# Second-layer weight sums of the MLP made by DMA in DRAM ahead of time, and one signal for each inner weight sum

## The reference

```
h    = rmsnorm(x); proj = h @ w_in
att  = sparse attention over the 256 best keys (prompt; sample with a paged cache)
rwkv = recurrent branch (delta-rule state, chunks of tokens)
x    = x + (sigmoid(gate_a) * (att @ w_branch_a) + sigmoid(gate_b) * (rwkv @ w_branch_b)) @ w_out
x    = x + square(relu(rmsnorm(x) @ w_mlp_in)) @ w_mlp_out        # 1024 -> 4096 -> 1024
y    = rmsnorm(x)
```

## Time and profile before

| | us |
|---|---|
| runs shown | 2499.18, 2497.75, 2504.57 (median 2499.18) |
| the profiled execution, its own time | 2501.81 |
| its span | 2500.0 |
| PE busy | 2294.0 (92%) |
| DVE busy | 1619.0 (65%) |
| ACT busy | 806.7 (32%) |
| POOL busy | 466.4 (19%) |
| DMA moved | 306.77 MB, mean 123 GB/s |

### The profile page before, as it was taken

One profiled execution on the slowest core, in us unless ns is written; L12 is line 12 of the kernel. 1 busy time (PEld: TensorE's weight loads), 2 busy tenths in 40 slices (PEclk: granted clock), 3 DMA queues, 4 the chain that ended last, 5 costly groups with the idle time before them and its releaser, 6 DMA issues. The chain is left out here.

```text
span 2500.0 us, 48830 instructions
## 1 busy us (share of the span) xinstructions
PE 2294.0 (92%) x19275; PEld 1709.7 (68%) x19275; DVE 1619.0 (65%) x3005; ACT 806.7 (32%) x1425; POOL 466.4 (19%) x354
## 2 busy tenths in 40 slices
PE   6999999999898999897999889999899999999986
PEld 4566788765656566665665668787687778778765
DVE  3257888964556564336557656648975785786787
ACT  4235888333343342224454432121121111111001
POOL 0020000000000000001101101034444544535441
PEclk8989999999999999899999999999999999999999
DMA  6441222443232313237877744506226325315302
GB/s 186 120 117 62 77 90 70 130 152 90 58 100 58 96 46 97 83 106 217 288 235 263 231 171 154 167 22 199 79 64 183 107 63 178 114 56 180 119 1 80
DMA packets 270656, 306.77 MB, mean 123 GB/s; under 512 B 56231, under 2 KB 183048, under 8 KB 270301
## 3 DMA queue, kind: packets, MB, share of 16 engines
q1 hardware_dynamic: 195316, 252.78, 32.0%
q10 hardware_dynamic: 75112, 50.87, 7.2%
HBM read 239.78 MB, written 62.23 MB: 121 GB/s over the span
## 5 line engine op out<-in xcount | busy, mean ns | idle before, releaser
L1286 PE MATMUL rwkv_banks<-gate_sides_then_att_T 128*128 128x384 f32 (+1 forms) x768 | 281.4, 499 | 8.4 <-PEq L441 3.7
L1286 PEld LDWEIGHTS rwkv_banks<-gate_sides_then_att_T 128*128 128x128 f32 x768 | 139.5, 197 | 77.1 <-issue 18.9
L3595 DVE TENSOR_TENSOR merged_then_hidden<-merged_then_hidden,ps_mm 128x544 f32<-128x544 f32 x180 | 127.5, 715 | 94.5 <-PE ps_mm L3320 94.5
L3320 PE MATMUL ps_mm<-gate_sides_then_att_T,w_mm 128*128 128x272 f32 x568 | 140.8, 397 | 10.1 <-issue 6.2
L600 PE MATMUL first_banks<-hT,w_pr 128*128 128x384 f32 (+3 forms) x432 | 144.3, 491 | 3.8 <-PEq L188 3.8
L910 DVE TENSOR_SCALAR_CACHE_REDUCE _and_tildes_then_k_pages<-scores,mid 128x384 f32<-128x384 f32 (+4 forms) x150 | 131.4, 876 | 3.1
L3320 PEld LDWEIGHTS ps_mm<-gate_sides_then_att_T,w_mm 128*128 128x128 f32 x568 | 108.6, 192 | 34.4 <-issue 7.0
L3402 ACT ACTIVATE merged_then_hidden<-merged_then_hidden 128x1088 f32<-128x1088 f32 x32 | 35.5, 1111 | 280.5 <-DVE merged_then_hidden L3607 280.5
L600 PEld LDWEIGHTS first_banks<-hT,w_pr 128*128 128x128 f32 (+1 forms) x432 | 81.1, 192 | 61.4 <-issue 20.5
L3320 PE MATMUL ps_mm<-gate_sides_then_att_T,w_sums_mm 128*128 128x272 f32 x400 | 101.3, 398 | 15.8 <-issue 6.8
L2376 POOL MEMSET gate_sides_then_att_T<- 128x136 f32 x1 | 0.2, 212 | 610.7 <-POOLq L1181 610.7
(11 more groups left out here) (619 smaller groups left out, 5289.4 us busy)
## 6 DMA issues: line engine op xcount, KB each, us to landing
v_pages<-in_cache_v SPq DMA_DIRECT2D x128, 256.0 KB, 5.3
gate_sides_then_att_T<-in_w_in ACTq DMA_DIRECT2D x46, 512.0 KB, 4.2
_and_tildes_then_k_pages<-in_cache_k SPq DMA_DIRECT2D x88, 256.0 KB, 3.4
gate_sides_then_att_T<-right_blocks_d SPq DMA_DIRECT2D x82, 272.0 KB, 2.8
right_blocks<-right_blocks_d SPq DMA_DIRECT2D x65, 272.0 KB, 2.7
T_and_gates_then_weights<-in_w_mlp_in SPq DMA_DIRECT2D x16, 1024.0 KB, 5.3
T_and_gates_then_weights<-in_w_mlp_out SPq DMA_DIRECT2D x16, 1024.0 KB, 5.4
w_pr<-in_w_in SPq DMA_DIRECT2D x27, 512.0 KB, 5.3
```

The source lines that it names most:

```text
L1286: ins = MM(B[:, gate_bank(n), 0:w], gw[:, n % 2, k_, :], hc[:, k_, 0:w], start=(k_ == 0), stop=(k_ == KO - 1))
L3320: ins = nc.tensor.matmul(ps[:, bank, 0:272], w, right[:, k, :], start=(k == 0 and step in f.OPENS), stop=(k == 1), skip_group_check=True)
L3595: V.tensor_tensor(to, of, f.pair(ps, q, step), ALU.add).then_inc(f.by_dve, 1)
```

## The change

**In the recurrent stage** POOL, behind its clears, issues 32 DMAs of 1 MB from DRAM to DRAM, four for each move, into a new DRAM tensor `sums_d`. 16 are copies, 16 add to what stands at the target (`accum_op`). They form s1 = a21 + a22, s3 = a21 + a11, s2 = s1 + a11 and s4 = s2 + a12 of `w_mlp_out` for all four rounds, in six groups with a wait for all moves so far between them, and a last wait behind them.

**In DOWN layers and TAIL** SP loads seven quarters in place of four, s1, s2, a21 (now s3) and s4 out of `sums_d`; VectorE makes no weight sums there. Since the DMAs only add, signs differ, and `spread_results` subtracts where it added before. In UP layers VectorE's four sums stay, in the order s1, s2, s3, s4 in place of s1, s3, s2, s4.

**UP's order** is P1, P2, P6, P7, P5, P4, P3, with P5 now ahead of P4; hidden blocks are finished in the order c11, c22, c21, c12 in place of c11, c21, c22, c12.

**Inner sums:** each of the four sets its own signal, and its step waits for it alone; each sum waits for the step of product q - 2 that last used its place. `inner_sums(1)` moves ahead of the last four additions of squares.

```diff
@@ -1261,6 +1261,34 @@
             ch.done(nc.gpsimd.memset(eps_gn[:, :], 64e-5))
             ch.done(nc.gpsimd.memset(xw[:, :, :], 0.0))
             p.clear_last(pool)
+            s1, s2, s3, s4 = (p.sums_d[n] for n in range(4))
+            w_2 = a["w_mlp_out"].rearrange("(r k c) (m e) -> k m r c e", k=2, c=512, m=2)
+            a11, a12, a21, a22 = w_2[0, 0], w_2[1, 0], w_2[0, 1], w_2[1, 1]
+
+            moved = [0]
+
+            def move(to, of, op):
+                for r in range(FF // D):
+                    if op is None:
+                        nc.gpsimd.dma_start(to[r], of[r]).then_inc(p.w_sums, 16)
+                    else:
+                        nc.gpsimd.dma_start(to[r], of[r], accum_op=op).then_inc(p.w_sums, 16)
+                moved[0] += 16 * (FF // D)
+
+            move(s1, a21, None)
+            move(s3, a21, None)
+            pool.wait_ge(p.w_sums, moved[0])
+            move(s1, a22, ALU.add)
+            move(s3, a11, ALU.add)
+            pool.wait_ge(p.w_sums, moved[0])
+            move(s2, s1, None)
+            pool.wait_ge(p.w_sums, moved[0])
+            move(s2, a11, ALU.add)
+            pool.wait_ge(p.w_sums, moved[0])
+            move(s4, s2, None)
+            pool.wait_ge(p.w_sums, moved[0])
+            move(s4, a12, ALU.add)
...
-    UP, DOWN, TAIL = (("P1", "P2", "P6", "P7", "P4", "P5", "P3"), ("P1", "P2", "P3", "P7", "P5", "P4", "P6"),
+    UP, DOWN, TAIL = (("P1", "P2", "P6", "P7", "P5", "P4", "P3"), ("P1", "P2", "P3", "P7", "P5", "P4", "P6"),
...
+    held = {**quarter, "s1": s1, "s2": s2, "s4": s4}
+    summed_before = ("s1", "s2", "a21", "s4")
...
-    target = {"P1": c11, "P6": c12, "P7": c22, "P4": c21, "P5": c12, "P2": c11, "P3": c12}
-    source = {"P7": c12, "P4": c22}
+    target = {"P1": c11, "P6": c12, "P7": c21, "P4": c21, "P5": c22, "P2": c11, "P3": c12}
+    source = {"P7": c12, "P5": c21}
...
-    hidden = [c[:, rows, :] for c in (c11, c21, c22, c12) for rows in (up, down)]
+    hidden = [c[:, rows, :] for c in (c11, c22, c21, c12) for rows in (up, down)]
...
-        if name in ("P1", "P4", "P2"):
-            n = {"P1": "a11", "P4": "a22", "P2": "a12"}[name]
-            if layer % 2:
-                eng.wait_ge(q_in[n], 16 * layer + 16)
-            else:
-                eng.wait_ge(q_scaled[n], 2 * layer + 4)
+        if layer % 2:
+            n = {"P1": "a11", "P4": "a22", "P2": "a12", "P5": "s1", "P6": "s2", "P7": "a21", "P3": "s4"}[name]
+            eng.wait_ge(q_in[n], 16 * (layer + 1 if n in quarter else (layer + 1) // 2))
+        elif name in ("P1", "P4", "P2"):
+            eng.wait_ge(q_scaled[{"P1": "a11", "P4": "a22", "P2": "a12"}[name]], 2 * layer + 4)
         else:
-            eng.wait_ge(l_summed, 4 * layer + {"P5": 1, "P7": 2, "P6": 3, "P3": 4}[name])
+            eng.wait_ge(l_summed, 2 * layer + {"P5": 1, "P6": 2, "P7": 3, "P3": 4}[name])
...
+                users = {"a11": "P1", "a12": "P2", "s4": "P3", "a21": "P7", "s1": "P5", "a22": "P4", "s2": "P6"}
                 for n in range(2 * R):
-                    for name, user, sums in (("a11", "P1", 3), ("a12", "P2", 4), ("a21", "P7", 2), ("a22", "P4", 1)):
+                    r = n // 2
+                    order = layers[n - 1] if n else UP
+                    for name in sorted(users if n % 2 else quarter, key=lambda name: order.index(users[name])):
                         if n:
-                            last = nth[n - 1][user]
+                            last = nth[n - 1][users[name]]
                             yield at(last, "P4") + STEP + 0.3
                             sp.wait_ge(*f.product(last, "P4"))
-                            sp.wait_ge(l_summed, 4 * (n - 1) + sums)
+                            if n % 2:
+                                sp.wait_ge(l_summed, 4 * r + {"a11": 3, "a12": 4}.get(name, 3))
                         else:
                             yield -90.0
                             sp.wait_ge(m_ready, 2 * H2)
                             sp.wait_ge(d.made, 14 * OUT)
-                        r, (k, m) = n // 2, corner[name]
-                        if n % 2:
+                        if n % 2 and name in summed_before:
+                            src = p.sums_d[summed_before.index(name), r]
+                        elif n % 2:
+                            k, m = corner[name]
                             src = w_2[r * D + 512 * k:r * D + 512 * k + 512, 512 * m:512 * m + 512]
                         else:
+                            k, m = corner[name]
                             src = w_1[512 * k:512 * k + 512, r * D + 512 * m:r * D + 512 * m + 512]
-                        sp.dma_start(quarter[name], src.rearrange("(k p) c -> p k c", p=128)).then_inc(q_in[name], 16)
+                        sp.dma_start(held[name], src.rearrange("(k p) c -> p k c", p=128)).then_inc(q_in[name], 16)
...
                 base, to = left[names[q]], inner[q % 2]
+
+                def free(step):
+                    if q >= 2:
+                        pool.wait_ge(*f.product(q - 2, step))
+
                 ready(pool, q)
-                if q >= 2:
-                    pool.wait_ge(*f.product(q - 2, "P4"))
-                else:
+                if q < 2:
                     pool.wait_ge(d.made, 14 * (OUT + 2 + 2 * q))
                 b11, b12, b21, b22 = base[:, 0:2, 0:256], base[:, 2:4, 0:256], base[:, 0:2, 256:512], base[:, 2:4, 256:512]
-                ch.done(G.tensor_tensor(to[:, 0, :, :], b21, b22, ALU.add))
-                ch.mark(G.tensor_tensor(to[:, 1, :, :], to[:, 0, :, :], b11, ALU.subtract))
-                ch.done(G.tensor_tensor(to[:, 2, :, :], b11, b21, ALU.subtract))
+                free("P5")
+                G.tensor_tensor(to[:, 0, :, :], b21, b22, ALU.add).then_inc(e_summed, 1)
+                free("P6")
+                pool.wait_ge(e_summed, 4 * q + 1)
+                G.tensor_tensor(to[:, 1, :, :], to[:, 0, :, :], b11, ALU.subtract).then_inc(e_summed, 1)
+                free("P3")
+                pool.wait_ge(e_summed, 4 * q + 2)
                 G.tensor_tensor(to[:, 3, :, :], b12, to[:, 1, :, :], ALU.subtract).then_inc(e_summed, 1)
+                free("P7")
+                G.tensor_tensor(to[:, 2, :, :], b11, b21, ALU.subtract).then_inc(e_summed, 1)
 
             for n in range(4 * H2):
                 if n == 4 * H2 - 4:
                     inner_sums(0)
+                    inner_sums(1)
                 pool.wait_ge(squared, n + 1)
                 if n >= 2:
                     pool.wait_ge(sq_added, n - 1)
                 t = (LO, HI)[n % 2]
                 G.tensor_tensor(rs[:, t], rs[:, t], squares[:, n % 2, :], ALU.add).then_inc(sq_added, 1)
-            for q in range(1, 14 * R):
+            for q in range(2, 14 * R):
...
-                    pe.wait_ge(e_summed, q + 1)
...
+                if step in sums:
+                    pe.wait_ge(e_summed, 4 * q + 1 + ("P5", "P6", "P3", "P7").index(step))
...
-                for n in range(2 * R):
-                    yield at(7 * n - 2, "P4") + STEP + 8.0 if n else -14.0
+                    dve.wait_ge(q_scaled[name], 2 * n + 4)
+
+                for n in range(0, 2 * R, 2):
+                    yield at(7 * n - 1, "P4") - 3.0 if n else -14.0
                     if n:
                         dve.wait_ge(*f.product(nth[n - 1]["P5"], "P4"))
                     else:
@@ -3545,23 +3590,23 @@
                     has(n, "a21")
                     has(n, "a22")
                     V.tensor_tensor(s1, a21, a22, ALU.add).then_inc(l_summed, 1)
-                    yield at(7 * n - 2, "P4") + STEP + 10.5 if n else 5.0
+                    yield at(7 * n - 1, "P4") + STEP + 0.9 if n else 7.0
                     has(n, "a11")
-                    dve.wait_ge(l_summed, 4 * n + 1)
-                    V.tensor_tensor(a21, a11, a21, ALU.subtract).then_inc(l_summed, 1)
-                    yield at(7 * n - 1, "P4") + STEP + 0.9 if n else 9.0
                     if n:
                         dve.wait_ge(*f.product(nth[n - 1]["P6"], "P4"))
                     else:
                         dve.wait_ge(d.made, 14 * ML)
+                    dve.wait_ge(l_summed, 2 * n + 1)
                     V.tensor_tensor(s2, s1, a11, ALU.subtract).then_inc(l_summed, 1)
-                    yield at(7 * n - 1, "P4") + STEP + 4.0 if n else 26.0
+                    yield at(7 * n - 1, "P4") + STEP + 6.0 if n else 12.0
+                    V.tensor_tensor(a21, a11, a21, ALU.subtract).then_inc(l_summed, 1)
+                    yield at(7 * n - 1, "P4") + STEP + 9.0 if n else 24.0
                     has(n, "a12")
                     if n:
                         dve.wait_ge(*f.product(nth[n - 1]["P3"], "P4"))
                     else:
                         dve.wait_ge(sq_added, 4 * H2)
-                    dve.wait_ge(l_summed, 4 * n + 3)
+                    dve.wait_ge(l_summed, 2 * n + 2)
...
+    p.sums_d = p.dram("sums_of_w_mlp_out_d", (4, FF // D, 512, 512))
```

39 lines of the change are left out of this document (20 added, 19 removed).

## The result

The changed kernel took 2548.5 us (median of four, 2543.6 to 2550.9) against 2498.5 for the kernel before: 1.019 times, with an interval of 1.0165 to 1.0216. It is 50 us slower. I had forecast 2478, with a range up to 2506. One execution of the run ml_alone (7677 us) and one of the kernel before (3840 us) were far slower than all others; every median and ratio here leaves them out.

The account below looks back on a forecast made before the run. PE was taken to pace the quarter products, with VectorE the bound in four UP to DOWN transitions. Terms -29 - 3 + 2.2 + 0 + 6 + 2 = -21.8 us gave 2478 us, range 2460 to 2506.

Parts of the forecast that it names:

- What the moves hit: Recurrent stage: gate loads take 6.7 us beside moves, four in the close stretch late by 1.45 each, 6 us lost.
- How long the moves take: Recurrent stage: 179 us counting adding moves double, 263 us with engines free for 0.68, ending at about 800.
- The rival that came true: Recurrent stage: moves choke gate loads, costing 4(L - 5.25) + (L - 8.4) + (L - 7.4) at load time L; chance 0.12.
- The transitions: Four UP to DOWN transitions: without VectorE's weight sums, 29 of PE's 38.9 us lost are won, bounds 20 and 37.
- the ceiling of 37.8: Four transitions: the most that removing VectorE's sums can win, 38.9 us less 1.1 still over in the last.
- I take 2.2 us lost in each transition: Four transitions: single operations before a gather and the new block order still cost PE 9 us in all.
- The second rival: Transitions: a chain of operations, not VectorE's load, ends PE's waits; 12 of 38.9 us come back, 2494; chance 0.12.
- One signal for each inner sum: Quarter products: PE's 3.2 us wait for the fourth POOL sum goes, 3 us won, bounds 1 and 4.
- inner_sums(1) ahead of the squares: Start of quarter products: new gap before P6 of product 0, old one before P5 of product 1 gone, 2.2 us lost.
- More loads in DOWN layers: Quarter products: 12 more loads of 1 MB cost 0, bounds 0 and 3.
- Later close pairs: Recurrent stage: the few close pairs of gate units after the close stretch lose 2 us, bounds 0 and 4.

Follow-up runs that it names:

- ml_alone: The changed kernel without its 32 moves, DOWN layers loading plain quarters in place of the sums: 2475.0 us, 0.990 times the kernel before.
- moves_single: The changed kernel with one move in flight at a time, POOL waiting for each before issuing the next: 1.006 times the kernel before.
- burst_later: The changed kernel with its moves begun only when 10 gate units are done, eight still in flight: 2523.6 us, 1.010 times the kernel before.
- spread: The paced kernel with the eight `hidden_sums` of a DOWN layer due 3.66 us apart in place of 0.9 (1.9 for the last round's last four): 2480.0 us.
- squares_first: The paced kernel with `inner_sums(1)` put back behind the last four additions of squares: 2492.5 us, 0.998 times the kernel before.
- paced: The changed kernel with one move in flight and one for each of gate units 10 to 41: 2492.6 us, 0.999 times the kernel before.
- after_load: The paced kernel with each move waiting for a gate load to have landed, not for a gate unit done: 2488.8 us, 0.996 times the kernel before.

## Why the prediction was wrong

- **What the moves hit** is the step that failed: "What does a load take beside a stream that never pauses? Nearest row: a 548 KB load issued right behind another of its size ... I take 6.7." It took 21.7 us. The row had one load ahead; the change has eight moves of 1 MB., 256 KB loads issued close together and landed after 10.1, was the nearer row, and I left it to a rival. Waits: 8 us forecast in the stage (6 and 2), 44.2 measured.
- **The clock** had no term in this stage. The first 1812 records kept PE busy 130.9 us at a granted clock of 0.80, before 112.7 at 0.96: 18 us more.
- **How long the moves take.** I shared the engines, "with the engines free for 0.68, 263 us". The moves took 180 us. That this is my 179 for engines that do nothing else is luck: that figure counts an adding move double, and it is a third dearer (moves_single). In the window of 195 us the moves' queue had 73.4% of the engines' time, some 143 us of all of them, and the other queues fell from 37.5% (525 to 720 us, kernel before) to 24.6%. So the moves did not take only what was left.
- **ScalarE's issues** had no term at all. I asked which queue stands behind POOL's waits, and not which engine stands in an issue when the DMA engines are full: 35.5 us in six issues of the changed kernel, which took 0.3 to 0.5 each before, and 21.3 us on PE's path in burst_later.
- **The rival that came true** was the choked loads, chance 0.12, with 2515 at a load of 13 us. Its formula at 21.7 us gives 66 + 13 + 14 = 93 us, and PE waited 44.2: presumably since a unit that comes late gives the next load more time. The kind was right. My highest price for the stage, 46 us, was a third below the 67.6 that it lost, since I took the load no further than 13 us and had neither the clock nor ScalarE's issues in it.
- **The transitions** gave 12.6 of 38.9 us and not 29. VectorE's load was the bound there, as I had read (40.4 us became 14.1 in the windows of the earlier trace rows), and the ceiling of 37.8 was sound: the spread kernel brings 29.9. The failed step is "I take 2.2 us lost in each transition": it was 2.6, 8.6, 8.0, 7.1, about half of it behind the windows. The working took VectorE's other operations to last as long as before, and the 32 `hidden_sums` grew from 42.0 to 63.5 us beside POOL's sums. I saw that "single operations in front of a gather" could be left, and did not look at VectorE's order, in which four of them stand with one gather between them. The second rival (12 us come back, "chain and not load") had the amount right, by luck, and the cause wrong: what is left is the row of `hidden_sums`, as the spread run shows. How much of it is their order and how much their new length no run parts.
- **One signal for each inner sum**: 3 us forecast; the three waits, 3.2 us in all, are gone. Right as far as it goes, but the term looked at no other engine: if it is these signals that bring POOL's sums beside `hidden_sums`, they cost more than they won.
- **inner_sums(1) ahead of the squares**: +2.2 forecast. The gap is where it was said, 5.4 us long and not 7.6; against squares_first it costs 2.9, against the kernel before 0.1 (53.1 for 53.0 us to the 200th record), since there the old gap was longer. Right in kind.
- **More loads in DOWN layers**: 0, and no wait of PE for one. **Later close pairs**: +2; the stage was 72 us behind at the 1812th record and 72 at the 3000th. Nothing, since the moves were over.
- As a sum: -29.8 for the quarter products was -15.1, +8 for the recurrent stage was +67.6, attention and the branches together gave -1.5, and what lies ahead and behind -3.1: +48 us in the profiled executions.

**Open.** Why moves for whose sake PE hardly waits for a load still cost 12 to 13 us. ScalarE's long issues in paced and after_load (3.0; 3.1 and 3.7 us) are some of it. The rest is in short waits of PE in the recurrence's chain ("issue", ahead of its products of 32x32: 12.5 to 14.4 us in place of 9.1 before); single executions of the same recurrent stage gave 618.5, 618.9, 622.2 and 631.6 us, so profiles of one execution can't settle it.

## What to carry to other kernels

An idle engine and DMA engines that are a third busy do not make a transfer free. Ask how much is in flight in front of the shortest load that an in-order engine waits for, and pace background transfers to one at a time, away from stretches where loads have no slack; that alone took the time from 1.019 to 0.999 of the kernel before, where no moves at all gave 0.990. When work is taken off a full engine, look next at the order of what remains: a row of long operations between short ones that others wait for cost PE 26 us here, and spreading it won 17 in the quarter products. And when an engine's work gets a new time, look at what runs beside it: the same VectorE sums took half as long again with POOL's sums beside them.

## What was not expected of the hardware

- A 512 KB load beside 1, 4 and 8 DRAM-to-DRAM moves of 1 MB each landed after 7.4, 16.2 and 21.7 us; alone after 4.2.
- The issue of a DMA on ScalarE's queue held ScalarE for up to 14.1 us; in the kernel before the longest of the stage took 1.6.
- A sum of 128x1088 elements on VectorE took 1.28 us with POOL idle beside it and up to 2.35 with an inner sum of POOL beside it.
- One at a time, most copying moves of 1 MB out of `w_mlp_out` took 6.6 to 7.5 us from one start to the next, most adding ones 9.5 to 9.7; adding is a third dearer, not double.
- A wait of PE of 2.7 us was followed by a step of 3.54 us in place of 2.00, and one of 2.97 us at another place by one of 2.10.
